# A transformer block with 32 experts: the down weights' loads move from SyncE's queue to ScalarE's

## What is computed

```
hgu  = xb @ w_gu[e] + b_gu[e]                # 1024 -> 2048
gate = minimum(hgu[:, :1024], 7); up = clip(hgu[:, 1024:], -7, 7)
act  = (up + 1) * gate * sigmoid(1.702 * gate)
y    = act @ w_down[e] + b_down[e]           # 1024 -> 1024
out  = zeros.at[tok].add(gate_of_token * y)
```

## Time and profile before

| | us |
|---|---|
| median of 3 runs | 1175.67 (1174.62 to 1176.19) |
| the profiled execution, its own time | 1174.33 |
| its span, first to last instruction | 1172.5 |
| TensorE busy | 1094.4 (93%) |
| VectorE busy | 260.5 (22%) |
| ScalarE busy | 140.5 (12%) |
| mean DMA rate over the span | 372 GB/s |

### The profile page before, as it was taken

The page is one execution under the profiler, slowest core; times in us unless marked ns, Lnnn a source line. Parts: engine busy times, 40 slices in busy tenths (PEclk is TensorE's granted clock), DMA queues, the critical chain, the costliest instruction groups (busy, mean ns, idle before and its releaser), DMA issues.

```text
span 1172.5 us, 11559 instructions
## 1 busy us (share of the span) xinstructions
PE 1094.4 (93%) x5084; PEld 469.0 (40%) x5084; DVE 260.5 (22%) x610; ACT 140.5 (12%) x242; POOL 9.8 (1%) x18
## 2 busy tenths in 40 slices
PE   7999999999999999999999989999999899999997
PEld 3677778543333333333333333333333233333332
DVE  1574323232111111111111112111111111111111
ACT  2315241010000000000000000000000000000000
POOL 1100000000000000000000000000000000000000
PEclk9999999989999999999999999999999999999999
DMA  8465646589999999999999999999999999999991
GB/s 268 148 224 216 241 150 256 213 362 428 426 424 426 426 425 425 426 426 425 426 425 425 426 424 425 426 423 427 425 424 425 427 424 425 427 425 424 428 383 63
DMA packets 53572, 435.68 MB, mean 372 GB/s; under 512 B 7216, under 2 KB 8400, under 8 KB 20656
## 3 DMA queue, kind: packets, MB, share of 16 engines
q1 hardware_dynamic: 53104, 434.30, 89.3%
q0 software_dynamic: 96, 0.08, 0.2%
q10 hardware_dynamic: 320, 0.53, 0.1%
HBM read 433.85 MB, written 1.05 MB: 371 GB/s over the span
## 4 chain that ended last, share of the span: by engine, by line
PE 52%; DMA 44%; DVE 2%; ACT 1%; issue 0%; SPq 0%; ACTq 0%; DVEq 0%
PE Pp L774 18%; DMA att<-in_w_down 16%; DMA G<-in_w_down 16%; PE Bp L789 9%; DMA XT<-in_w_down 7%; PE Pp L495 7%; DMA qkv<-in_w_down 5%; PE Pp L483 3%; PE Ap L803 2%; PE Pp L663 2%; PE Ap L674 2%; PE Bp L760 2%; PE Pp L522 1%; PE Bp L781 1%; DMA unit<-in_w_in 1%; DVE G L1251 1%
## 5 line engine op out<-in xcount | busy, mean ns | idle before, releaser
L774 PE MATMUL Pp<-ring,OBT 128*64 128x512 f32 x1360 | 301.0, 592 | 0.0
L1240 DVE TENSOR_SCALAR G<-Pp 128x512 f32<-128x512 f32 x32 | 22.1, 691 | 680.0 <-PE Pp L774 680.0
L774 PEld LDWEIGHTS Pp<-ring,OBT 128*64 128x64 f32 x1360 | 97.0, 137 | 186.4 <-issue 182.8
L774 PE MATMUL Pp<-unit,OBT 128*64 128x512 f32 x448 | 100.9, 592 | 0.0
L495 PE MATMUL Pp<-XT,unit 128*128 128x256 f32 x384 | 85.2, 380 | 0.0
L495 PEld LDWEIGHTS Pp<-XT,unit 128*128 128x128 f32 x384 | 72.1, 190 | 10.9 <-issue 1.1
L1439 ACT ACTIVATE G<-G 128x512 f32<-128x512 f32 x32 | 20.2, 630 | 451.0 <-DVE G L1240 451.0
L803 PE MATMUL Ap<-G,cst 64*128 64x512 f32 x264 | 65.6, 615 | 1.4 <-ACT G L1446 1.4
L789 PE MATMUL Bp<-G 128*64 128x512 f32 x200 | 49.9, 620 | 15.3 <-DMA G<-in_w_down 14.8
L789 PE MATMUL Bp<-att,G 128*64 128x512 f32 x208 | 49.9, 600 | 11.0 <-DMA att<-in_w_down 10.5
L789 PE MATMUL Bp<-qkv,G 128*64 128x512 f32 x208 | 49.9, 600 | 10.8 <-DMA qkv<-in_w_down 10.3
(11 more groups left out here) (214 smaller groups left out, 799.6 us busy)
## 6 DMA issues: line engine op xcount, KB each, us to landing
ring<-in_w_gate_up SPq DMA_DIRECT2D x85, 2048.0 KB, 32.4
unit<-in_w_gate_up SPq DMA_DIRECT2D x28, 2048.0 KB, 31.1
more<-in_w_gate_up SPq DMA_DIRECT2D x15, 2048.0 KB, 31.8
XR<-in_w_down SPq DMA_DIRECT2D x26, 1024.0 KB, 30.0
qkv<-in_w_down SPq DMA_DIRECT2D x26, 1024.0 KB, 30.0
att<-in_w_down SPq DMA_DIRECT2D x26, 1024.0 KB, 30.0
G<-in_w_down SPq DMA_DIRECT2D x25, 1024.0 KB, 30.0
XT<-in_w_down SPq DMA_DIRECT2D x25, 1024.0 KB, 30.0
```

The costliest lines, as they stand in the source:

```text
L774: last = mm((Gps, Ups)[q // 2][64 * (q % 2):64 * (q % 2) + 64, :], xT[:, k % 4, k // 4, :], w[:, q * 512:(q + 1) * 512], start=False, stop ...
L1240: V.tensor_scalar(gm, Gps, LIMIT, None, ALU.min).then_inc(d_gm, 1)
```

## The change

The four down loads of an expert leave SyncE's list. ScalarE issues them on its own queue, right behind the result copy L1446, with no wait of their own: the copy has waited for `m_y`, which says that all four buffers are free. The three `dn_used` increments per expert go. SyncE's list has the gate/up turns only, with the waits that they had. The first five down pieces (turns 0 to 4) stay where they were, on SyncE.

```diff
-        gu_used, dn_used = sem("gu_used"), sem("dn_used")
+        gu_used = sem("gu_used")
...
-            def dn_released(turn):
-
-                e0, s0 = divmod(turn - SINGLES, DN)
-                if s0 == DN - 1:
-                    sp.wait_ge(m_y, e0 + 1)
-                else:
-                    sp.wait_ge(dn_used, e0 * (DN - 1) + s0 + 1)
-
             def load_behind(e):
 
                 for turn in range(GU * e + PAIRS, min(GU * (e + 1) + PAIRS, GU * NE)):
                     gu_released(turn)
                     load_gu(*divmod(turn, GU))
-                for turn in range(DN * e + SINGLES, min(DN * (e + 1) + SINGLES, DN * NE)):
-                    dn_released(turn)
-                    load_dn(*divmod(turn, DN))
...
                 for s in range(4):
                     last = down(dn_piece(e, s), s)
-                    last.then_inc(m_y if s == 3 else dn_used, 1)
+                    if s == 3:
+                        last.then_inc(m_y, 1)
...
                 act.wait_ge(m_y, e + 1)
                 A(ysb, Yps, ACT.Copy).then_inc(a_y, 1)
+                for turn in range(DN * e + SINGLES, min(DN * (e + 1) + SINGLES, DN * NE)):
+                    act.dma_start(singles[turn % SINGLES], dn_src(*divmod(turn, DN))).then_inc(
+                        single_full[turn % SINGLES], 16)
```

## The result

The changed kernel takes 1194.19 us (median of 4 runs, 1194.03 to 1194.88), the kernel before beside it 1175.14 us. The ratio is 1.0163, with a 95% interval of 1.0145 to 1.0181: 19 us slower. Run again beside the experiments it took 1190.6 us against 1174.41, a ratio of 1.0142 (1.0125 to 1.0159). The forecast was 1189.0, 14.7 us more than before.

The account below looks back on a forecast made before the run. Full DMA engines, 29.5 us per expert, were taken as the mid-run bound. The first seven cycles become 26.35 + 28.0 + 5 x 29.5 = 201.9 instead of 187.2 us, so 1174.33 + 14.7 = 1189.0 us; range 1171 to 1200.

Parts of the forecast that it names:

- The lead is not used: First seven expert cycles: gate/up pieces lie too early in full buffers; 201.9 instead of 187.2 us, 14.7 us more.
- Turns by packets, a third of the bytes: Both load queues full: they alternate by packets, 16 KB gate/up against 8 KB down; a down piece takes 7.4 us, not 2.46.
- The wait lies at the fourth piece only: TensorE waits for loads only at each expert's fourth down piece, some 3.2 us.
- SyncE's queue has work throughout: TensorE frees four gate/up buffers per cycle and SyncE's queue carries four, keeping cycles locked at 29.5 us.
- The DMA idles behind the first expert and before the last: DMA idle from 269 to 273 us, 4.3 us lost once, and again between the last experts.
- A median landing near 25 us: Sign for the forecast: down loads on ScalarE's queue land near 25 us in the median.
- Issue 1.0 us behind `m_y`: All four down loads go out some 1.0 us behind `m_y`: copy 0.60, issue 0.41.
- 1189.0: Forecast time in us of the changed kernel: 1174.33 + 14.7, from the profiled execution; chance 0.63.
- Rival (a): Down gets more than a third of the bytes; TensorE later waits for gate/up; 1173.8 us, no change; chance 0.22.
- Rival (b): Turns between the load queues cost DMA time; at 0.05 us each, 3 us on 29 cycles, 1280 us; chance 0.05.
- Rival (c): Loop of issue, transfer, landing and matmuls is longer; landing of 5 us or more gives 30 us cycles, 1203; chance 0.07.
- Rival (d): The change does nothing, because the lead at the start has no value; 1174.3 us; chance 0.03.

Follow-up runs that it names:

- the second trace: The changed kernel run again with no edit: 1190.6 us median, its profiled execution 1187.66 us.
- the run with equal packets: The changed kernel with each 2 MB gate/up piece loaded as two transfers, so both queues have 8 KB packets: 1182.7 us.
- the two kernels with equal packets: Gate/up pieces halved to 8 KB packets, in the changed kernel (1182.7 us) and in the kernel before with all loads on SyncE's queue (1182.5 us).

## Why the prediction was right, point by point

*The lead is not used.* Right, in place and in size: seven cycles of 202.6 and 201.7 us in two traces, forecast 201.9, the third of them 31.0 and 29.5. The stretch from copy 1 to copy 2 was put at 28.0; it took 28.06 and 27.88. That it fits to 0.1 us is partly luck: 28.0 was taken between 27.3 and 28.8 without a row that decides. What TensorE lost in a cycle before is read rightly as some 3.2 us, but the 107.4 us put beside it are another quantity: the earlier trace rows counts the waits of the weight loads, some 4.9 us a cycle.

*Turns by packets, a third of the bytes.* Right. It was read from stores of 2 KB, and from their counts alone, 37 to 35, which do not prove turns of one packet; the order of the records does, for the loads of 16 and 8 KB. The two ways of changing the ratio, half the gate/up packet and half the down packet, move the time in the direction that the ratio says, the second by 22 us more than expected. The rule of the Trainium skill (DMA: Bandwidth & Descriptors, Queues, rings and completion order) that an engine drains some 9 to 17 descriptors from one queue before it turns is not borne out by these loads: 57 of 59 pairs of packets changed the queue.

*The wait lies at the fourth piece only.* Right, 1.49 and 2.94 us in the rows above. *SyncE's queue has work throughout.* Nearly: it ran empty from 545 to 549 us, where the down queue had 95.5% of the engines' time and the DMA stayed full, and in a few other places. *The DMA idles behind the first expert and before the last.* Right, but the first hole was put at 4.3 us and is 2.7, some 2.5 in the second trace. *A median landing near 25 us.* Wrong: 19.8. It was a sign and no term of the sum; why the loads land earlier was not traced.

*Issue 1.0 us behind `m_y`.* Wrong in the kernel's favour, and without weight: ScalarE starts the transfer at 276.61, 0.01 us after its copy has started, and nothing in the program makes it wait for the copy's end.

*1189.0.* The sum for the profiled execution gave a span of 1187.2; the second trace has 1185.9, the first 1193.1, of which 4.3 us lie ahead of the first copy and were in no term. The two medians are 19.1 and 16.2 us above the kernel before; 14.7 was forecast. The term that was missing is the length of the slow-clock stretch at 240 us, which differs between executions and holds up the first expert and with it the first loads. That is shown for the profiled executions alone, the slowest of the first four and the fastest of the second.

*Rival (a)*, more than a third: did not happen, but the run with equal packets shows its course, nine cycles at 26.3 us and then waits for gate/up. Its time was put at 1173.8; 1182.7 less the 10.5 us of the lower rate (378.5 MB at 421 instead of 426 GB/s) is 1172.2, an estimate. *Rival (b)*, a price for turning: excluded by the mid-run rate of the changed kernel and by the two kernels with equal packets. *Rival (c)*, a longer loop: excluded here by 29.7 us a cycle, and what it describes happens with packets of 4 KB. *Rival (d)*: excluded by the cycles themselves.

The sentence that the lead "stays in the buffers" has the best part of the case in it. It holds for the kernel before too, and reversing the order of issue on one queue from expert 12 or 20 on takes 10 us out.

## What to carry to other kernels

Where the DMA is the bound and the buffers start full, look at which loads TensorE waits for and which lie there early: here the order among the loads, at the same rate, decided whether that lead was ever used, and it could be used once, late in the run, at no cost. While both are full, the two queues share by packets, so the queue with the longer rows gets the larger part; before a stream goes to a queue of its own, compare the row bytes of the streams, which set their shares, with the bytes that each has to move, and look at the time that a batch has until it is needed. Here the ratio of the packets equalled the ratio of the bytes, which left no slack at all.

## What the runs showed that was not expected

Halving the packets of either stream, from 16 to 8 KB for gate/up or from 8 to 4 KB for down, took the rate of one full queue from 426 to 421 GB/s and cost some 8 to 10 us; each packet more costs its engine some 11 ns.

One wait of some 3 us often costs TensorE its clock where three shorter ones did not. In the changed kernel, a wait of 3.02 us and the windows around it:

```profile
625.58 3.34 PE L778 MATMUL Bp<-qkv,G 128*64 128x512 f32 x8 [3.02 <-DMA qkv<-in_w_down]
```

```profile
622.00:626.00 4.00, 0.97 (x6) 0.30 (x4) 0.00 (x0) 0.00 (x0) 0.00 (x0) 0.88 1.00 424
625.00:629.00 4.00, 3.42 (x12) 1.10 (x14) 0.00 (x0) 0.04 (x1) 0.00 (x0) 0.57 1.02 430
```

The granted clock falls to 0.57 in the second, most of it at 1.2 GHz, after the engine had been busy for 0.97 of 4 us; the eight matmuls there take 3.34 us instead of 1.94. Not every such wait does it: of the fifteen of 2.67 to 4.51 us in this trace eleven are followed by a slow group of matmuls and four are not (one of 3.05 us at 684.70 is not), and none of the nine shorter ones is, 0.64 to 1.71 us. What tells the four from the eleven was not found. The mean clock of the span fell from 0.996 to 0.977. In the cycles this costs nothing that shows, 29.77 against 29.73 us. A likely reason, not tested, is that the down queue is still busy with the piece before, so that a later `m_y` delays no load.
